# A macaron transformer stack in split fp32 on one core: all low parts of the weights made on VectorE

## The reference

```python
def macaron_half_ffn(x, pre_g, post_g, w_gate, w_up, w_down):
    h = rmsnorm(x, pre_g)
    h = (jax.nn.silu(h @ w_gate) * (h @ w_up)) @ w_down
    return x + 0.5 * rmsnorm(h, post_g)
```

## Time and profile before

| what | value |
|---|---|
| time, median of 3 runs | 4013.93 us (4011.29 to 4030.01) |
| the profiled execution, its own time | 4018.81 us |
| its span | 4017.0 us |
| mean granted clock of PE | 0.876 |
| PE busy | 3344.4 us, 83% |
| DVE busy | 1874.9 us, 47% |
| ACT busy | 1522.4 us, 38% |
| POOL busy | 1089.2 us, 27% |
| HBM read | 479.27 MB |

### The profile page before, as it was taken

How to read it: one execution, slowest core, us unless ns; L and a number is a source line. 1 busy time by engine, 2 the same in 40 slices (tenths; PEclk the granted TensorE clock), 3 DMA queues, 4 the chain that set the end, 5 groups by cost and what they waited for, 6 DMA issues and landing times.

```text
span 4017.0 us, 63475 instructions
## 1 busy us (share of the span) xinstructions
PE 3344.4 (83%) x26994; PEld 3172.4 (79%) x26994; DVE 1874.9 (47%) x3171; ACT 1522.4 (38%) x2521; POOL 1089.2 (27%) x518
## 2 busy tenths in 40 slices
PE   8987899978889999898678998988126989966898
PEld 8986799976779999797477898987116989954798
DVE  5444454548545453656333434543003545443353
ACT  4432344434124444464434444433003434432343
POOL 2220122222332222222011222221784222220122
PEclk9986899989889999899679999988558989976799
DMA  6531254544004555334023454532002534510253
GB/s 209 169 132 48 100 173 156 185 137 157 3 28 163 168 164 185 117 111 137 32 100 126 137 184 132 168 127 89 11 16 95 174 121 148 174 67 21 69 174 116
DMA packets 131721, 484.42 MB, mean 121 GB/s; under 512 B 14703, under 2 KB 14847, under 8 KB 130607
## 3 DMA queue, kind: packets, MB, share of 16 engines
q1 hardware_dynamic: 129456, 470.25, 35.9%
q0 software_dynamic: 1984, 10.12, 0.8%
HBM read 479.27 MB, written 1.05 MB: 120 GB/s over the span
## 4 chain that ended last, share of the span: by engine, by line
PE 65%; DVE 11%; ACT 10%; issue 8%; POOL 5%; DMA 0%; DVEq 0%; SPq 0%; POOLq 0%; ACTq 0%
PE ps L174 64%; ACT hi L171 5%; POOL yT L154 3%; ACT arena L171 2%; DVE lo L154 2%; PE ps L182 2%; DVE yT L162 1%; DVE tmp L154 1%; DVE arena L154 1%; POOL small L154 1%; ACT L171 1%; DVE arena L162 1%; DVE tmp L162 1%; DVE sq L154 1%; DVE small L168 1%
## 5 line engine op out<-in xcount | busy, mean ns | idle before, releaser
L154 DVE TENSOR_TENSOR lo<-raw,hi 128x1024 fp32r<-128x1024 f32 x595 | 888.0, 1497 | 1162.1 <-ACT hi L171 1161.4
L174 PE MATMUL ps<-hh,hi 128*128 128x256 f32 (+1 forms) x4624 | 1365.1, 295 | 67.1 <-DVE hl L162 38.2
L154 POOL TENSOR_TENSOR lo<-raw,hi 128x1024 fp32r<-128x1024 f32 x297 | 723.6, 2436 | 2360.9 <-ACT hi L171 2360.9
L174 PE MATMUL ps<-hl,hi 128*128 128x256 f32 (+1 forms) x4624 | 1344.9, 291 | 0.0
L174 PE MATMUL ps<-hh,lo 128*128 128x256 f32 (+1 forms) x4624 | 1344.6, 291 | 0.0
L171 ACT ACTIVATE hi<-raw 128x1024 fp32r<-128x1024 f32 x892 | 928.5, 1050 | 579.6 <-PE ps L174 573.4
L174 PEld LDWEIGHTS ps<-hh,hi 128*128 128x128 f32 x4624 | 908.3, 196 | 92.6 <-DVE hl L162 33.5
L174 PEld LDWEIGHTS ps<-hl,hi 128*128 128x128 f32 x4624 | 907.1, 196 | 0.6
L174 PEld LDWEIGHTS ps<-hh,lo 128*128 128x128 f32 x4624 | 907.3, 196 | 0.0
L174 PE MATMUL ps<-hfh,hi 128*128 128x256 f32 (+1 forms) x1760 | 503.7, 286 | 30.2 <-DVE tmp L154 30.2
L174 PE MATMUL ps<-hfh,lo 128*128 128x256 f32 (+1 forms) x1760 | 502.3, 285 | 0.0
(11 more groups left out here) (308 smaller groups left out, 3321.3 us busy)
## 6 DMA issues: line engine op xcount, KB each, us to landing
raw<-in_l_ffn_w_gate SPq DMA_DIRECT2D x88, 512.0 KB, 3.6
raw<-in_l_ffn_w_up SPq DMA_DIRECT2D x88, 512.0 KB, 3.7
raw<-in_l_ffn_w_down SPq DMA_DIRECT2D x88, 512.0 KB, 3.5
raw<-in_g SPq DMA_DIRECT2D x88, 512.0 KB, 3.5
raw<-in_u SPq DMA_DIRECT2D x88, 512.0 KB, 3.5
raw<-in_d SPq DMA_DIRECT2D x88, 512.0 KB, 3.5
raw<-in_ffn_w_gate SPq DMA_DIRECT2D x44, 512.0 KB, 4.3
raw<-in_ffn_w_up SPq DMA_DIRECT2D x44, 512.0 KB, 4.3
```

The costliest lines, as they stand in the source:

```text
L154: return self.e.tensor_tensor(o, a, b, op)
L174: return self.e.matmul(o, a, b, start=first, stop=final, skip_group_check=loose)
```

## The change

The method `lo_pool`, its 24 calls, the semaphore `cvp` and the test on w % 3 are taken out. `W.lo` makes every unit, at the places where it was already called, and `need` waits on the one semaphore left. ACT's list and SP's list stay as they are. POOL keeps the powers, its share of the residual additions and of some mixers, and the loads of tables and parameters.

```diff
@@ -196,8 +196,8 @@
-        self.cvh, self.cvl, self.cvp, self.done = [K.sem(n) for n in ("cvh", "cvl", "cvp", "wdone")]
-        self.at_act = self.at_dve = self.at_pool = 0
+        self.cvh, self.cvl, self.done = [K.sem(n) for n in ("cvh", "cvl", "wdone")]
+        self.at_act = self.at_dve = 0
@@ -234,21 +234,11 @@
     def lo(self, dve, upto):
         for w in range(self.at_dve, min(upto, len(self.units))):
-            if w % 3 != 2:
-                self.low(dve, w).then_inc(self.cvl, 1)
+            self.low(dve, w).then_inc(self.cvl, 1)
             self.at_dve = w + 1
 
-    def lo_pool(self, pool, upto):
-        for w in range(self.at_pool, min(upto, len(self.units))):
-            if w % 3 == 2:
-                self.low(pool, w).then_inc(self.cvp, 1)
-            self.at_pool = w + 1
-
     def need(self, pe, w):
-        if w % 3 == 2:
-            pe.wait_ge(self.cvp, w // 3 + 1)
-        else:
-            pe.wait_ge(self.cvl, w - w // 3 + 1)
+        pe.wait_ge(self.cvl, w + 1)
@@ -897,16 +882,12 @@
     def pool(self, pool):
         K, W, u = self.K, self.K.W, self.u
         self.entry.pool(pool)
-        W.lo_pool(pool, u + 8)
         if self.lazy:
             self.entry.norm.power(pool)
         for j in range(NF):
-            W.lo_pool(pool, u + max(2 * j + 7, 9))
             if j == 2 and u == 0:
                 K.enter.tables(pool)
-        self.down.pool(pool)
         self.exit.pool(pool)
-        W.lo_pool(pool, self.next + 5)
...
@@ -3032,10 +2994,7 @@
         for j in range(24):
             if j == 1:
                 self.entry.pool(pool)
-            W.lo_pool(pool, self.u + j + 6)
-        self.down.pool(pool)
         self.exit.pool(pool)
-        W.lo_pool(pool, self.next + 5)
...
@@ -3946,7 +3898,6 @@
         @block.gpsimd
         def _(_):
             k.enter.pool(pool)
-            k.W.lo_pool(pool, 5)
             for s in made[1:]:
                 s.pool(pool)
             store.pool(pool)
```

More of the change, by code:

```diff
@@ L796, in dve @@
             self.K.W.lo(dve, self.u + k + 6)
-    def pool(self, pool):
-        for k in range(self.nk - 3):
-            self.K.W.lo_pool(pool, self.u + k + 6)
 class Ffn:
@@ L2025, in pool @@
         self.entry.pool(pool)
-        W.lo_pool(pool, self.u + 18)
         pool.wait_ge(*self.l1(2))
         self.pk.load(pool)
-        W.lo_pool(pool, self.u + 24)
         pool.wait_ge(*self.l2(7))
@@ L2034, in pool @@
         self.pn.load(pool)
-        W.lo_pool(pool, self.u + 29)
         self.ticks(lambda i, s: self.pool_hop(pool, i, s))
-        self.down.pool(pool)
         self.exit.pool(pool)
-        W.lo_pool(pool, self.next + 5)
     def pool_hop(self, pool, i, s):
```

## The result

| kernel | median | range | ratio to before, 95% interval |
|---|---|---|---|
| before | 4013.49 us | 4011.29 to 4030.01 | |
| the change | 4126.43 us | 4125.77 to 4129.13 | 1.0274 [1.0246, 1.0301] |

The change makes the kernel 113 us slower, inside the range of 4060 to 4138, and 24 us over the forecast of 4102. The profiled execution has a span of 4124.0 us against 4017.0, +107.

The account below looks back on a forecast made before the run. It took PE and the DVE-ACT relay of the lazy Ffns as nearly level at 5.7 us a round. Terms 101 + 8 − 13 − 8 = +88 gave 4102 us on the median, range 4060 to 4138.

Parts of the forecast that it names:

- term 1: Rounds of the eight lazy Ffns: each lengthens to 6.32 us, or 6.39 with 272 tokens; +101 us in sum.
- Term 2: PE's clock after the up phase: a 10 us wait slows the four 272-token down phases; +8 us.
- Term 3: Stage boundaries: three DVE low parts take 3.5 us without POOL's, and POOL's loads go earlier; −13 us.
- I take that it slips in again: Stage boundaries: POOL's power gets in behind DVE's first low part, through in 1.61 us in the earlier trace.
- the sign that I had named: Stage boundaries: `small` on POOL waiting for all three DVE low parts would show the boundary estimate wrong.
- the reading as a queue: Stage boundaries: three low parts issued back to back keep POOL out, making the sum +101 instead of +88.
- Term 4: Mixers: each avoided collision saves 2.2 us against 1.14 for an added DVE low part; eight places, −8 us.
- Term 5: The rest, non-lazy Ffns and loads that POOL issues: no effect, since PE or the raw ring covers them.
- A: Faster: collisions are the real price and lazy Ffn rounds reach 5.67 us or less; −35 us, 3979; chance 0.06.
- B: Lazy Ffn rounds are 6.32 us only early, later say 6.0; +41 us, 4055; chance 0.11.
- C: PE's clock drops within the up phase, a fifth of rounds at 1.2 GHz; 150 us more, 4250; chance 0.05.
- D: No difference: the added 365 us sit in DVE's idle time, PE covers the relay; within 0.5%; chance 0.04.

Follow-up runs that it names:

- experiment 1: Kernel before, with DVE making the low parts of the lazy Ffns' rounds and POOL the other 186 of its 297: 4144.68 us, ratio 1.0325.
- experiment 2: Kernel before, with POOL keeping its low parts in the lazy Ffns' rounds and DVE making all others: 4013.72 us, ratio 0.9995.
- experiment 3: Changed kernel, with both `hi` of a lazy Ffn round moved earlier in ACT's list, ahead of silu and `hfh`: 3971.83 us, ratio 0.9896.
- experiment 5: Changed kernel, with only `hi`(2j+5) moved ahead of the silu in ACT's list: 3971.38 us, ratio 0.9875.
- experiment 4: Kernel before, POOL's low parts kept, with both `hi` moved earlier in ACT's list as in experiment 3: 3962.10 us, ratio 0.9874.
- the second pair: Second profiles of both kernels, unedited: before 4020.08 us, ratio 0.9995; the change 4124.38 us, ratio 1.0241.
- experiment 7: Kernel of experiment 3, with DVE waiting for POOL's powers at 272 tokens and Mem's copy of V before the last low part: 3956.60 us, ratio 0.9839.

## Why the prediction was right, and where it was not

**The mechanism (term 1) held to 1%**: +101.6 for +101. The round with both low parts and a silent POOL existed in the trace before, once in an Ffn, and every round took its length. Experiments 1 and 2 show that the loss is at this place, and that the other places sum to nothing; 3 and 5 show that the wait for `hi` is the cause, not DVE's work.

**Term 2 held**: the wait of 10 us measured 9.8, and the down phases of 272 tokens lost 9.4 us in one pair and 5.8 in the other, for +8. With the wait gone (experiments 3 and 4) the loss is gone. The size is rough: without the long wait these four still differ by 1.7 us between the two profiles of before and are 2.8 longer in experiment 2.

**Term 3 was mis-sized, −13 for −3 to −6.** Its first half was better than I said: −1.7 at each of four boundaries instead of −1.0, since DVE's first low part there had also waited 0.61 for its `hi` and the one it makes first now does not; and the loads gave −4.6 (−3.1 in the second pair) and −2.4, for −2.4 each. But four other boundaries of 256 tokens, where DVE had two low parts and now has three, got 0.2 to 0.6 us longer. The step that failed is "I take that it slips in again". It does with 256 tokens:

```profile
234.32 3.49 DVE L154 TENSOR_TENSOR lo<-raw,hi 128x1024 fp32r<-128x1024 f32 x3
```

```profile
234.49 1.63 POOL L154 TENSOR_TENSOR small<-small,cst 128x2 f32<-128x2 f32 x1 [198.70 <-DVE small L159]
```

1.63 us, as the 1.61 of the earlier trace rows. With 272 tokens it does not: at nine places, five boundaries and four entries of Ffns, the first of the two powers takes 3.89 us and ends behind all three low parts (experiment 7). That is the sign that I had named for this term being wrong. The five boundaries got 1.1 to 1.8 us longer: +7. The upper bound I gave for this case (0 for the term) covered it. So the reading as a queue, which I had set against it, fits the 272 tokens and not the 256. Why the power gets in behind the first low part in one case and not in the other stays open.

**Term 4 had the wrong sign outside Nsa.** I charged a low part in a mixer with 1.14 us and credited 2.2 for a collision. In Rwkv and Mem the added low part brought the same wait for a late `hi` that I had found in the Ffns: +8.0 and +5.8 (+10.3 and +2.1 in the second pair). The step was "against 1.14 for one more low part on DVE": the price of an instruction in a queue includes the wait in front of it, and I applied that to one stage only. Nsa's −12 (−9 in the second pair) was in no term; without it the forecast would have missed by more, so that much of it is luck.

**Term 5, put at nothing, was −4.8 and −7.7.** Of it, 3.5 and 2.9 us lie between the boundary after Rwkv and the first round of the next Ffn; the rest is in pieces that no run sorts out. So the +19 over the forecast of +88 are +0.6, +1.6, +7.4, +14.1 and −4.8: the terms outside the rounds were out by more than their sum shows.

**Of the rivals** A (faster) fell with the first round: 6.32, not 5.67. What it had right is that the collisions cost DVE 156 us and vanished; they were not on the path. B fell as well, the rounds are 6.32 from the third to the last (PE may be four pairs ahead, not the two that I wrote there). C did not occur: in stretches of 10 us the clock was 1.00 through all eight up phases of the first profile. D fell with A.

## What to carry to other kernels

Before work is moved to an idle engine, or back, read what that engine does just before it at that place. Here a low part costs 1.23 us as work and nothing in most stages, but behind a result that another engine was told to make too late it holds up a ping-pong of two engines. The cheaper cure was in neither the old nor the new owner: make the input earlier. Two lines of ACT's list gave 54 us in the kernel before and 155 in the changed one.

## What the runs showed of the hardware

- A POOL power of 128x2 begun 0.16 us after the first of two or three DVE subtractions issued back to back, each with two SBUF inputs, took 1.60 to 1.63 us with 256 tokens. With 272 tokens, where a second power follows it, it took 3.89 us behind three (nine places) and 2.75 to 2.77 behind two (three places of the kernel before; 1.61 and 1.62 at two others). Undisturbed it takes 0.71, the second one 0.54. What decides between the two stays open.
- The same 128x128 matmuls of Nsa, 94 to 96 of them, took 10 us at a granted clock of 1.00 in some kernels and 20 us at 0.50 in others, with PE busy throughout and busy for at least 10 us before. What sets the drop off there stays open.
- Two profiles of one kernel differ by up to 8.5 us in a single mixer and by 0.1 us in all the rounds together.
